# Order of the routing's bookkeeping ahead of the experts: one turn, the ranks, the slot list and the weights are moved

## The chip, the cores and the metric

One core of a Trainium2 chip runs the whole program. The metric is the device time of one execution in microseconds. Three executions of the kernel before gave 2938.93, 2939.79 and 2942.79 us.

## What is computed

Two transformer blocks in float32 on 1024 tokens of width 1024. The second block ends in a hierarchical mixture of experts: 4 groups of 8 experts, the best group for each token, in it the two best experts, 32 experts in all. Cut to what the change touches:

```python
x = x + jnp.matmul(merged, w_out[l])
h2 = rms_norm(x, ffn_norm_g[l])
g_logits = matmul(hf, w_rg) + b_rg ; g_sel = argmax(g_logits)
e_logits = (matmul(hf, w_re) + b_re) of the chosen group
top_p, top_i = lax.top_k(softmax(e_logits), 2)
wts = top_p / sum(top_p) * g_w ; eidx = g_sel * 8 + top_i
# each expert gets its tokens in order, in blocks of 128 rows
row_tok[dest] = token ; row_w[dest] = weight
yb = (silu(xb @ w_g[e]) * (xb @ w_u[e])) @ w_d[e] * wb[:, None]
y.at[row_tok].add(yb)
```

## The kernel before

The order of the work is written out by hand: each stage gives every engine its own program, and semaphores tie them together. Each engine works through its program in order. The change is in one stage, `phase_out_route` (line 2391 on), which lies between the dense products of the second block and the expert stage.

Tokens come in 8 tiles of 128 (TT = 8). For each tile t, TensorE multiplies the merged activations by `w_out` in two halves of 512 columns, `multiply(t, 0)` and `multiply(t, 1)` (L2698 to L2700, 24 matmuls each, in 3 parts for accuracy). VectorE adds the residual (`residual`, L2474) once both halves are there. ScalarE squares and sums (L2659) and takes a root (L2662) in `square(t)`; VectorE finishes the norm (L2486). TensorE turns the normed tile by 8 transposes (`turn(t)`, L2714), ScalarE copies the result out of PSUM (`place(t)`, L2669), and TensorE multiplies it by the router's weights (`logit(t)`, L2723, 16 instructions of 36 columns). On ScalarE `place(t - 1)` stands behind `square(t)`.

VectorE chooses group and experts from the logits for tiles 0 to 4, 5 and 6, and 7, in three calls of `choose`. Its marks are kept in `both` (which experts a token takes) and `run` (sums over tiles). Then:

- The ranks: TensorE multiplies `both` by the triangular `before` (L2742) and `run` by `ones` (L2744), both over 8 x 32 = 256 columns, and sums up the last of `run` (L2747). From these VectorE works out each token's row in its expert's block: `dest`, split into `place_f` and `block_f` (L2467 at 2293.61 us to L2573).
- The weights: five small operations on 8 or 32 elements (L2575 to L2579) that need two exponentials of ScalarE (L2683, L2684).
- The list of slots: 16 one-hot tables `at_place` (128 columns) and a table `told` of 2 x 48 columns for each, which holds the token number (columns 0 to 47) and the token's weight (48 to 95). VectorE builds them in two halves of 8. TensorE multiplies them (L2752, 16 products of 96 columns, 32 instructions in the trace), and VectorE turns the result into `slot_token`, `slot_row` and `slot_weight` (L2596 to L2602). Ahead of that VectorE works out which experts need a further block (`extra_expert`, L2590 to L2594).
- GpSimd waits for `slots` and gathers the rows of the first two experts (L2647).

The expert stage follows in the same programs without a barrier. An expert needs three matrices of 2 MB, each loaded in two halves into one buffer for its kind (gate, up, down). ScalarE rounds a half (L3044), VectorE takes the remainder (L3109, in `lo(GATE)`, `lo(UP)`, `lo(DOWN)`), and this frees the half for the next load (L2769, issued by SyncE). TensorE turns the gathered rows (L2968), ScalarE rounds them (L3060), VectorE takes the remainder (`lo_x`, L3124), and the products follow (L2959). For the first expert the order is:

```python
# VectorE                    # ScalarE              # TensorE
lo(GATE)(0, 0)               hi(GATE)(0, 0)         turn_x(0, 0)
lo_x(0, 0)                   hi_x(0, 0)             product(0, 0, GATE, opened)
lo(UP)(0, 0)                 hi(UP)(0, 0)           product(0, 0, UP, hidden)
```

Of the kernel before, what the change touches and what calls it, by code (L numbers as in the profile page):

```python
# [20 lines left out]
ALU = mybir.AluOpType  # L21
AX = mybir.AxisListType

P = 128
SEQ = 1024
D = 1024
TT = SEQ // P
# [27 lines left out]
NE = NG * EPG  # L55
DE = D // 2
ASSIGN = 2 * SEQ
EXTRA = ASSIGN // P
# [2332 lines left out]
def phase_out_route(c, merged, w_high, w_low, x1_dram, x2, gain_dram, xn_dram, keep_dram, w_group,  # L2391
# [5 lines left out]
    nc = c.nc  # L2397
# [50 lines left out]
    GROUPS_OF = ((0, 5), (5, 7), (7, 8))  # L2448
    logit_bank = lambda t: 7 if t in (5, 6) else 6
    ranks, total = t3(c.ps[:, 0, 0:TT * NE]), c.ps[:, 0, TT * NE:(TT + 1) * NE]  # L2450
    with c.stage(within) as (ctx, block):
        S = lambda n: c.sem(ctx, "or_" + n)
        x_in, params = [S("x_in0"), S("x_in1")], S("params")
# [9 lines left out]
        def _(dve):  # L2463
# [75 lines left out]
            for i in range(TT):  # L2539
# [4 lines left out]
                if i == TT - 2:  # L2544
                    choose(*GROUPS_OF[0])
            choose(*GROUPS_OF[1])
            choose(*GROUPS_OF[2])
            at_step["chosen"] = st.n

            tt(gexp, grp[:, :, 0:NG], gtop[:, :, 0:1].to_broadcast([P, TT, NG]), ALU.subtract)  # L2550
            tt(e2.unsqueeze(2), top[:, :, 1:2], top[:, :, 0:1], ALU.subtract)
# [19 lines left out]
            ts(c.block_no, c.dest, 7, None, ALU.arith_shift_right, ALU.bypass)  # L2571
            W(V.tensor_copy(place_f, c.place_no))
            W(V.tensor_copy(block_f, c.block_no))  # L2573
            dve.wait_ge(act_step, 2)
            W(V.tensor_reduce(gsum, gexp, AX.X, ALU.add))  # L2575
            ts(s2, e2, 1.0, None, ALU.add, ALU.bypass)
            tt(s2, s2, gsum, ALU.mult)
            W(V.reciprocal(c.weight[:, 0:TT], s2))
            tt(c.weight[:, TT:NJ], c.weight[:, 0:TT], e2, ALU.mult)  # L2579
            for j in range(2):  # L2580
                half = slice(j * TT, (j + 1) * TT)
                tt(at_place[:, half, :], bt(iota_f), bl(place_f[:, half], P), ALU.is_equal)
                tt(in_block[:, half, :], bt(iota_f[:, 0:NBLK]), bl(block_f[:, half], NBLK),
                   ALU.is_equal)
                tt(told[:, half, 0:NBLK], in_block[:, half, :], bl(row_f[:, half], NBLK), ALU.mult)
                tt(told[:, half, NBLK:2 * NBLK], in_block[:, half, :], bl(c.weight[:, half], NBLK),
                   ALU.mult)
                at_step["told", j] = st.n

            tt(cmp_, bl(bno, NE), bt(upto, EXTRA), ALU.is_ge)  # L2590
            W(V.tensor_reduce(bex, cmp_, AX.X, ALU.add))
            ts(bex, bex, float(NE - 1), None, ALU.min, ALU.bypass)
            W(V.tensor_copy(c.extra_expert, bex))
            W(V.tensor_copy(c.extra_count, upto[:, NE - 1:NE]))  # L2594
            dve.wait_ge(listed, 1)
            rows = c.ps[:, 1, 0:NBLK]  # L2596
            ts(wrapped, rows, float(SEQ - EMPTY), float(-SEQ), ALU.is_ge, ALU.mult)
# [1 line left out]
                                   op0=ALU.add, op1=ALU.add).then_inc(slots, 1)  # L2599
            W(V.scalar_tensor_tensor(out=c.slot_row, in0=wrapped, scalar=float(EMPTY), in1=rows,  # L2600
                                     op0=ALU.add, op1=ALU.add))
            W(V.tensor_copy(c.slot_weight, c.ps[:, 1, NBLK:2 * NBLK]))  # L2602

        @block.sync
        def _(sp):
# [81 lines left out]
        def _(pe):  # L2687
# [17 lines left out]
            def turn(t):  # L2705
                pe.wait_ge(ready, t + 1)
                for h in range(2):
                    if t:
                        pe.wait_ge(placed, 2 * t + h - 1)
                    else:  # L2710
                        pe.wait_ge(dense.by_vec, EVICTED)
                    for k in range(4):
                        kk = 4 * h + k
                        mm = nc.tensor.transpose(c.ps[:, 4 + h, k * P:(k + 1) * P],  # L2714
                                                 xn[t % 2][:, kk * P:(kk + 1) * P], c.ident[:])
                    mm.then_inc(turned, 1)

            def logit(t):
                pe.wait_ge(placed, 2 * t + 2)
                if t == 0:  # L2720
                    pe.wait_ge(params, 80)
                for k in range(KC):
                    mm = nc.tensor.matmul(c.ps[:, logit_bank(t), t * NL:(t + 1) * NL],  # L2723
                                          hT[:, k, :], w[:, k, :],
                                          start=(k == 0), stop=(k == KC - 1))
                mm.then_inc(logits, 1)

            pe.wait_ge(retired, 1)
            for t in range(TT):
                multiply(t, 0)  # L2730
                if t >= 2:
                    logit(t - 2)
                multiply(t, 1)
                if t:
                    turn(t - 1)
            logit(TT - 2)
            turn(TT - 1)
            logit(TT - 1)
            pe.wait_ge(step, at_step["chosen"])
            for used in experts_may:  # L2740
                pe.sem_inc(used, 1)
            nc.tensor.matmul(c.ps[:, 0, 0:TT * NE], c.before[:], both.rearrange("p t n -> p (t n)"),  # L2742
                             start=True, stop=False, skip_group_check=True)
            nc.tensor.matmul(c.ps[:, 0, 0:TT * NE], c.ones[:],  # L2744
                             run[:, 0:TT].rearrange("p t n -> p (t n)"), start=False, stop=True,
                             skip_group_check=True)
            nc.tensor.matmul(total, c.ones[:], run[:, TT], start=True, stop=True,  # L2747
                             skip_group_check=True).then_inc(ranked, 1)
            for n in range(NJ):
                if n % TT == 0:  # L2750
                    pe.wait_ge(step, at_step["told", n // TT])
                mm = nc.tensor.matmul(c.ps[:, 1, 0:2 * NBLK], at_place[:, n, :], told[:, n, :],  # L2752
                                      start=(n == 0), stop=(n == NJ - 1))
            mm.then_inc(listed, 1)


# [826 lines left out]
```

## Time and profile before

| | us |
|---|---|
| median of three executions | 2939.79 |
| the profiled execution, its own time | 2932.78 |
| its span | 2931.0 |
| TensorE busy | 2756.0 |
| VectorE busy | 1907.3 |
| ScalarE busy | 1442.8 |
| GpSimd busy | 529.9 |
| mean granted TensorE clock | 0.976 |

Times in the trace are microseconds from the start of the span. A granted clock of 1.00 is 2.4 GHz, 0.50 is 1.2 GHz. The routing stage's products run from 2171 to 2275 us, the bookkeeping to about 2310 us, the experts from there to the end. A bracket at the end of a timeline row is how long the engine was idle ahead of it and who released it. Matmuls overlap, so the length of a merged row is from its first start to its last modelled end.

### The profile page before, as it was taken

How to read it: one execution, taken by the hardware profiler on the slowest of the kernel's cores; microseconds unless marked ns; L12 is line 12 of the kernel's file. 1: busy time of each engine (PE TensorE's matmuls, PEld its weight loads, DVE VectorE, ACT ScalarE, POOL GpSimd, SP SyncE). 2: the span in 40 equal slices, each digit the busy share in tenths (PEclk: the TensorE clock that was granted, in tenths of full speed). 3: DMA queues.
4: the chain of work that ended last, by engine and by line, in shares of the span. 5: the costliest groups of instructions: out<-in, count | busy, mean ns of one | idle time of the engine just before them, and what ended most of it. 6: DMA issues, size and time to landing. Idle time of an engine off the chain costs nothing.

```text
span 2931.0 us, 35753 instructions
## 1 busy us (share of the span) xinstructions
PE 2756.0 (94%) x13268; PEld 2251.2 (77%) x13278; DVE 1907.3 (65%) x2187; ACT 1442.8 (49%) x2117; POOL 529.9 (18%) x397
## 2 busy tenths in 40 slices
PE   7999999999998999999989998899899699999997
PEld 6788887888876776887878876778678588888875
DVE  4776836344454664345543987899863699888985
ACT  4444436323336665434333356533532377777774
POOL 0002300000006775001000000000110144334332
PEclk9999999999999999999999998999999799999998
DMA  4110011313456663131211100111222699999995
GB/s 104 44 49 9 16 53 36 108 43 108 165 168 141 153 146 83 44 108 51 87 58 53 44 29 1 30 44 50 93 97 86 226 385 376 371 364 370 363 361 178
DMA packets 162600, 387.92 MB, mean 132 GB/s; under 512 B 72321, under 2 KB 72449, under 8 KB 137888
## 3 DMA queue, kind: packets, MB, share of 16 engines
q1 hardware_dynamic: 151920, 369.13, 37.5%
q0 software_dynamic: 9216, 16.81, 2.3%
q8 instruction: 90, 1.47, 0.2%
q10 hardware_dynamic: 1328, 0.14, 0.0%
q14 instruction: 46, 0.38, 0.0%
HBM read 347.93 MB, written 54.85 MB: 137 GB/s over the span
## 4 chain that ended last, share of the span: by engine, by line
PE 51%; DMA 12%; DVE 10%; POOL 6%; ACT 5%; issue 4%; POOLq 0%; DVEq 0%; SPq 0%; ACTq 0%; PEldq 0%
PE ps L897 12%; PE ps L899 12%; PE ps L898 12%; DMA ex_raw<-in_w_down_e 10%; POOL fa_pl L1336 6%; PE ps L2959 3%; DVE ex_w L3109 3%; DMA ex_raw<-in_w_up_e 2%; ACT ex_w L3044 2%; PE ps L2698 1%; PE ps L1741 1%; PE ps L2700 1%; PE ps L1743 1%; PE ps L1742 1%; PE ps L2699 1%
## 5 line engine op out<-in xcount | busy, mean ns | idle before, releaser
L3109 DVE TENSOR_TENSOR ex_w<-ex_raw,ex_w 128x2048 fp32r<-128x2048 f32 x190 | 430.7, 2289 | 63.4 <-ACT ex_w L3044 61.0
L3044 ACT ACTIVATE ex_w<-ex_raw 128x2048 fp32r<-128x2048 f32 x190 | 362.0, 1916 | 112.9 <-DMA ex_raw<-in_w_up_e 56.8
L2959 PE MATMUL ps<-ex_w,ex_xT 128*128 128x512 f32 x1536 | 367.6, 395 | 13.7 <-DVE ex_xT L3124 13.4
L2959 PEld LDWEIGHTS ps<-ex_w,ex_xT 128*128 128x128 f32 x1536 | 286.9, 189 | 79.5 <-issue 15.1
L1003 DVE TENSOR_TENSOR bs_t<-arena,bs_t 128x1024 fp32r<-128x1024 f32 x88 | 107.8, 1225 | 269.4 <-ACT bs_t L956 269.4
L956 ACT ACTIVATE bs_t<-arena 128x1024 fp32r<-128x1024 f32 x88 | 93.3, 1061 | 294.1 <-PE ps L899 280.3
L793 DVE SCALAR_TENSOR_TENSOR arena<-arena,small 128x1023 f32<-128x1023 f32 (+9 forms) x168 | 213.4, 1271 | 3.5
L1336 POOL TENSOR_TENSOR fa_pl<-fa_p,fa_ph 128x512 fp32r<-128x512 f32 x192 | 196.4, 1041 | 82.0 <-ACT fa_ph L1474 80.4
L2959 PE MATMUL ps<-ex_w,ex_hT 128*128 128x512 f32 x768 | 184.5, 396 | 0.3 <-issue 0.2
L897 PE MATMUL ps<-bs_t,bs_w 128*128 128x512 f32 x448 | 175.3, 391 | 7.8 <-DVE bs_w L994 4.3
L898 PE MATMUL ps<-bs_t,bs_w 128*128 128x512 f32 x448 | 174.4, 389 | 0.0
L899 PE MATMUL ps<-bs_t,bs_w 128*128 128x512 f32 x448 | 174.3, 389 | 0.0
L2959 PEld LDWEIGHTS ps<-ex_w,ex_hT 128*128 128x128 f32 x768 | 143.0, 189 | 30.4 <-issue 1.3
L897 PE MATMUL ps<-gb_t,gb_w 128*128 128x512 f32 x368 | 146.9, 399 | 15.9 <-DVE gb_w L994 8.1
L1003 DVE TENSOR_TENSOR za_t<-arena,za_t 128x1024 fp32r<-128x1024 f32 x48 | 60.1, 1252 | 142.5 <-ACT za_t L956 142.4
L1524 DVE TENSOR_REDUCE small<-ps 128x1 f32<-128x512 f32 (+1 forms) x192 | 100.7, 553 | 78.7 <-PE ps L1361 43.3
L897 PE MATMUL ps<-za_t,za_w 128*128 128x512 f32 x368 | 145.0, 394 | 5.6 <-DVE za_t L1003 3.3
L899 PE MATMUL ps<-gb_t,gb_w 128*128 128x512 f32 x368 | 145.3, 395 | 0.0
L898 PE MATMUL ps<-gb_t,gb_w 128*128 128x512 f32 x368 | 145.1, 394 | 0.0
L898 PE MATMUL ps<-za_t,za_w 128*128 128x512 f32 x368 | 144.2, 392 | 0.0
L899 PE MATMUL ps<-za_t,za_w 128*128 128x512 f32 x368 | 143.9, 391 | 0.0
L1464 ACT ACTIVATE fa_p<-ps 128x512 f32<-128x512 f32 x192 | 94.3, 491 | 88.3 <-PE ps L1401 42.0
(422 smaller groups left out, 6568.2 us busy)
## 6 DMA issues: line engine op xcount, KB each, us to landing
ex_raw<-in_w_gate_e SPq DMA_DIRECT2D x64, 1024.0 KB, 13.7
ex_raw<-in_w_up_e SPq DMA_DIRECT2D x64, 1024.0 KB
ex_raw<-in_w_down_e SPq DMA_DIRECT2D x64, 1024.0 KB, 13.6
arena<-in_w_in SPq DMA_DIRECT2D x108, 512.0 KB, 3.7
att_qk<-bs_split SPq DMA_DIRECT2D x8, 2048.0 KB, 10.8
fa_a<-att_qk SPq DMA_DIRECT2D x32, 256.0 KB
fa_b<-att_qk SPq DMA_DIRECT2D x16, 512.0 KB, 6.5
arena<-in_w_out SPq DMA_DIRECT2D x16, 512.0 KB, 7.1
```

Source lines behind the costliest of these rows:

```text
L793: ins = dve.scalar_tensor_tensor(out=acc[:, b, back:], in0=src[:, b, 0:SEQ - back], scalar=w, in1=acc[:, b, back:], op0=ALU.mult, op1=ALU.add)
L897: nc.tensor.matmul(c.ps[:, t, :], a[0], b[0], start=(k == 0), stop=False)
L898: nc.tensor.matmul(c.ps[:, t, :], a[0], b[1], start=False, stop=False)
L899: mm = nc.tensor.matmul(c.ps[:, t, :], a[1], b[0], start=False, stop=(n == last[j]))
L956: nc.scalar.activation(tp[s][0], jobs[j][0][:, k, :], ACT.Identity).then_inc(t_high, 1)
L1003: V.tensor_tensor(tp[s][1], jobs[j][0][:, k, :], tp[s][0].bitcast(F32), ALU.subtract)\
L1336: nc.gpsimd.tensor_tensor(low[x % 4][:, 0:w], prob[x % 3][:, 0:w], f32(high[x % 4][:, 0:w]), ALU.subtract).then_inc(lowered, 1)
L1464: nc.scalar.activation(prob[x % 3][:, 0:w], c.ps[:, S_BANK[x % 3], 0:w], ACT.Exp)\
L1524: V.tensor_reduce(to, c.ps[:, M_BANK[z % 2], 0:width], AX.X, ALU.max, negate=True)\
L2959: mm = nc.tensor.matmul(out, l, r, start=(k == 0 and n == 0), stop=(k == kc - 1 and n == 2))
L3044: nc.scalar.activation(half_of(part[m][0], h), raw[m][:, h * W // 2: (h + 1) * W // 2], ACT.Identity).then_inc(high[m], 1)
L3109: V.tensor_tensor(half_of(part[m][1], h), raw[m][:, h * W // 2: (h + 1) * W // 2], half_of(as_f32(part[m][0]), h), ALU.subtract)\
```

## The change

`turn(6)` is issued ahead of `multiply(7, 1)` rather than behind it. The rank products are split: tiles 0 to 6 (224 columns) as soon as `choose(5, 7)` is done, tile 7 (32 columns) and the total after `choose(7, 8)`. The five operations for the weights go behind the tables, which are built without the weights. TensorE multiplies the tables twice: first with the 48 columns of token numbers, into bank 1, later with the 48 columns of weights, into bank 7. VectorE makes `slot_token` and `slot_row` after the first, then multiplies the weights into `told`, works out the extra experts, waits for the second listing and copies `slot_weight`.

```diff
--- before.py
+++ after.py
@@ -2448,6 +2448,7 @@
     GROUPS_OF = ((0, 5), (5, 7), (7, 8))
     logit_bank = lambda t: 7 if t in (5, 6) else 6
     ranks, total = t3(c.ps[:, 0, 0:TT * NE]), c.ps[:, 0, TT * NE:(TT + 1) * NE]
+    WEIGHTS = 7
     with c.stage(within) as (ctx, block):
         S = lambda n: c.sem(ctx, "or_" + n)
         x_in, params = [S("x_in0"), S("x_in1")], S("params")
@@ -2544,8 +2545,9 @@
                 if i == TT - 2:
                     choose(*GROUPS_OF[0])
             choose(*GROUPS_OF[1])
+            at_step["chosen", 0] = st.n
             choose(*GROUPS_OF[2])
-            at_step["chosen"] = st.n
+            at_step["chosen", 1] = st.n
 
             tt(gexp, grp[:, :, 0:NG], gtop[:, :, 0:1].to_broadcast([P, TT, NG]), ALU.subtract)
             tt(e2.unsqueeze(2), top[:, :, 1:2], top[:, :, 0:1], ALU.subtract)
@@ -2571,27 +2573,19 @@
             ts(c.block_no, c.dest, 7, None, ALU.arith_shift_right, ALU.bypass)
             W(V.tensor_copy(place_f, c.place_no))
             W(V.tensor_copy(block_f, c.block_no))
+            halves = [slice(j * TT, (j + 1) * TT) for j in range(2)]
+            for j, half in enumerate(halves):
+                tt(at_place[:, half, :], bt(iota_f), bl(place_f[:, half], P), ALU.is_equal)
+                tt(in_block[:, half, :], bt(iota_f[:, 0:NBLK]), bl(block_f[:, half], NBLK),
+                   ALU.is_equal)
+                tt(told[:, half, 0:NBLK], in_block[:, half, :], bl(row_f[:, half], NBLK), ALU.mult)
+                at_step["told", j] = st.n
             dve.wait_ge(act_step, 2)
             W(V.tensor_reduce(gsum, gexp, AX.X, ALU.add))
             ts(s2, e2, 1.0, None, ALU.add, ALU.bypass)
             tt(s2, s2, gsum, ALU.mult)
             W(V.reciprocal(c.weight[:, 0:TT], s2))
             tt(c.weight[:, TT:NJ], c.weight[:, 0:TT], e2, ALU.mult)
-            for j in range(2):
-                half = slice(j * TT, (j + 1) * TT)
-                tt(at_place[:, half, :], bt(iota_f), bl(place_f[:, half], P), ALU.is_equal)
-                tt(in_block[:, half, :], bt(iota_f[:, 0:NBLK]), bl(block_f[:, half], NBLK),
-                   ALU.is_equal)
-                tt(told[:, half, 0:NBLK], in_block[:, half, :], bl(row_f[:, half], NBLK), ALU.mult)
-                tt(told[:, half, NBLK:2 * NBLK], in_block[:, half, :], bl(c.weight[:, half], NBLK),
-                   ALU.mult)
-                at_step["told", j] = st.n
-
-            tt(cmp_, bl(bno, NE), bt(upto, EXTRA), ALU.is_ge)
-            W(V.tensor_reduce(bex, cmp_, AX.X, ALU.add))
-            ts(bex, bex, float(NE - 1), None, ALU.min, ALU.bypass)
-            W(V.tensor_copy(c.extra_expert, bex))
-            W(V.tensor_copy(c.extra_count, upto[:, NE - 1:NE]))
             dve.wait_ge(listed, 1)
             rows = c.ps[:, 1, 0:NBLK]
             ts(wrapped, rows, float(SEQ - EMPTY), float(-SEQ), ALU.is_ge, ALU.mult)
@@ -2599,7 +2593,17 @@
                                    op0=ALU.add, op1=ALU.add).then_inc(slots, 1)
             W(V.scalar_tensor_tensor(out=c.slot_row, in0=wrapped, scalar=float(EMPTY), in1=rows,
                                      op0=ALU.add, op1=ALU.add))
-            W(V.tensor_copy(c.slot_weight, c.ps[:, 1, NBLK:2 * NBLK]))
+            for half in halves:
+                tt(told[:, half, NBLK:2 * NBLK], in_block[:, half, :], bl(c.weight[:, half], NBLK),
+                   ALU.mult)
+            at_step["weighted"] = st.n
+            tt(cmp_, bl(bno, NE), bt(upto, EXTRA), ALU.is_ge)
+            W(V.tensor_reduce(bex, cmp_, AX.X, ALU.add))
+            ts(bex, bex, float(NE - 1), None, ALU.min, ALU.bypass)
+            W(V.tensor_copy(c.extra_expert, bex))
+            W(V.tensor_copy(c.extra_count, upto[:, NE - 1:NE]))
+            dve.wait_ge(listed, 2)
+            W(V.tensor_copy(c.slot_weight, c.ps[:, WEIGHTS, 0:NBLK]))
 
         @block.sync
         def _(sp):
@@ -2725,32 +2729,44 @@
                                           start=(k == 0), stop=(k == KC - 1))
                 mm.then_inc(logits, 1)
 
+            def rank(a, b):
+                out = c.ps[:, 0, a * NE:b * NE]
+                nc.tensor.matmul(out, c.before[:], both[:, a:b].rearrange("p t n -> p (t n)"),
+                                 start=True, stop=False, skip_group_check=True)
+                nc.tensor.matmul(out, c.ones[:], run[:, a:b].rearrange("p t n -> p (t n)"),
+                                 start=False, stop=True, skip_group_check=True)
+
             pe.wait_ge(retired, 1)
             for t in range(TT):
                 multiply(t, 0)
                 if t >= 2:
                     logit(t - 2)
+                if t == TT - 1:
+                    turn(TT - 2)
                 multiply(t, 1)
-                if t:
+                if 1 <= t < TT - 1:
                     turn(t - 1)
             logit(TT - 2)
             turn(TT - 1)
             logit(TT - 1)
-            pe.wait_ge(step, at_step["chosen"])
+            pe.wait_ge(step, at_step["chosen", 0])
+            rank(0, TT - 1)
+            pe.wait_ge(step, at_step["chosen", 1])
             for used in experts_may:
                 pe.sem_inc(used, 1)
-            nc.tensor.matmul(c.ps[:, 0, 0:TT * NE], c.before[:], both.rearrange("p t n -> p (t n)"),
-                             start=True, stop=False, skip_group_check=True)
-            nc.tensor.matmul(c.ps[:, 0, 0:TT * NE], c.ones[:],
-                             run[:, 0:TT].rearrange("p t n -> p (t n)"), start=False, stop=True,
-                             skip_group_check=True)
+            rank(TT - 1, TT)
             nc.tensor.matmul(total, c.ones[:], run[:, TT], start=True, stop=True,
                              skip_group_check=True).then_inc(ranked, 1)
             for n in range(NJ):
                 if n % TT == 0:
                     pe.wait_ge(step, at_step["told", n // TT])
-                mm = nc.tensor.matmul(c.ps[:, 1, 0:2 * NBLK], at_place[:, n, :], told[:, n, :],
+                mm = nc.tensor.matmul(c.ps[:, 1, 0:NBLK], at_place[:, n, :], told[:, n, 0:NBLK],
                                       start=(n == 0), stop=(n == NJ - 1))
+            mm.then_inc(listed, 1)
+            pe.wait_ge(step, at_step["weighted"])
+            for n in range(NJ):
+                mm = nc.tensor.matmul(c.ps[:, WEIGHTS, 0:NBLK], at_place[:, n, :],
+                                      told[:, n, NBLK:2 * NBLK], start=(n == 0), stop=(n == NJ - 1))
             mm.then_inc(listed, 1)
 
 
```

## Rows read from the trace of the kernel before

**Rows 1.** The page of the profile, its first line.

```profile
span 2931.0 us, 35753 instructions
```

**Rows 2.** The chain that ended last: start, length, what.

```profile
2275.27 1.24 DVE arena L2474
...
2278.01 1.07 ACT arena L2669 x2
...
2310.80 4.42 DMA arena<-expert_in,ints
...
2319.62 8.38 PE ps L2959 x24
...
2328.51 1.92 ACT ex_w L3044
...
2342.95 5.50 PE ps L2959 x24
```

**Rows 3.** Timeline of TensorE, 2267 to 2311 us: start, length, what, idle before.

```profile
2267.72 1.87 PE L2723 MATMUL ps<-arena 128*128 128x36 f32 x16
...
2275.00 1.04 PE L2714 MATMUL ps<-ident,arena 128*128 128x128 f32 x8
2279.13 2.07 PE L2723 MATMUL ps<-arena 128*128 128x36 f32 x16 [3.09 <-ACT arena L2669]
...
2283.64 3.63 PE L2723 MATMUL ps<-arena 128*128 128x36 f32 x16 [0.69 <-ACT arena L2669]
2291.20 1.19 PE L2742 MATMUL ps<-arena,before 128*128 128x256 f32 x2 [3.93 <-DVE arena L2467]
...
2293.03 0.47 PE L2747 MATMUL ps<-arena,ones 128*128 128x32 f32 x2
2302.93 6.30 PE L2752 MATMUL ps<-arena 128*128 128x96 f32 x32 [9.42 <-DVE arena L2467]
```

**Rows 4.** Timeline of VectorE, 2293 to 2320 us.

```profile
2293.61 0.39 DVE L2467 TENSOR_TENSOR arena<-ps,arena 128x224 f32<-128x224 f32 x1 [2.43 <-PE ps L2747]
...
2298.80 0.19 DVE L2575 TENSOR_REDUCE arena<-arena 128x8 f32<-128x32 f32 x1
...
2299.87 2.41 DVE L2467 TENSOR_TENSOR arena<-arena 128x1024 f32<-128x1024 f32 x3
2302.31 0.56 DVE L2467 TENSOR_TENSOR arena<-arena,small 128x384 f32<-128x384 f32 x1
...
2305.94 0.69 DVE L2467 TENSOR_TENSOR arena<-arena 128x512 f32<-128x512 f32 x1
...
2309.93 0.21 DVE L2602 COPY small<-ps 128x48 f32<-128x48 f32 x1
2311.04 4.49 DVE L3109 TENSOR_TENSOR ex_w<-ex_raw,ex_w 128x2048 fp32r<-128x2048 f32 x2 [0.90 <-DVE small L2602]
2318.34 1.23 DVE L3124 TENSOR_TENSOR ex_xT<-ps,ex_xT 128x1024 fp32r<-128x1024 f32 x1 [2.80 <-ACT ex_xT L3060]
```

**Rows 5.** Busy time by stretch: busy us of each engine, granted clock, DMA share, GB/s.

```profile
2281.00:2282.00 1.00, 1.00 (x6) 1.00 (x7) 0.66 (x5) 0.00 (x0) 0.03 (x1) 0.50 1.10 315
...
2308.00:2309.00 1.00, 1.00 (x10) 1.00 (x9) 0.00 (x0) 0.00 (x0) 0.00 (x0) 0.91 0.00 0
...
2319.00:2324.00 5.00, 4.38 (x10) 3.47 (x11) 4.43 (x3) 4.18 (x3) 0.38 (x1) 0.50 0.88 329
```

**Rows 6.** Timeline of SyncE's queue, loads of the expert weights.

```profile
2313.36 2.53 SPq L2769 DMA_DIRECT2D ex_raw<-in_w_gate_e  x2
...
2332.77 2.53 SPq L2769 DMA_DIRECT2D ex_raw<-in_w_gate_e  x2
```

**Rows 7.** Busy time by stretch in the expert stage, columns as in rows 5.

```profile
2330.00:2340.00 10.00, 7.57 (x38) 6.26 (x37) 9.03 (x6) 7.88 (x6) 1.64 (x2) 1.00 0.62 213
2340.00:2350.00 10.00, 10.00 (x51) 8.46 (x51) 10.00 (x6) 7.85 (x7) 0.00 (x0) 1.00 1.00 406
...
2400.00:2500.00 100.00, 100.00 (x475) 83.88 (x474) 91.68 (x57) 75.02 (x55) 45.04 (x22) 1.00 1.00 376
```

## Prediction

> **What bounds the kernel now.** I read the chain that ended last first, then the timelines of TensorE and VectorE around it, then clock and DMA by stretch. Up to 2275 us TensorE is the chain: it multiplies without a gap. From 2275.27 to 2328 us the chain is a relay between engines [rows 2]: residual on VectorE, square and copy on ScalarE, logits and turn on TensorE, `choose` on VectorE, ranks on TensorE (2291.20 to 2293.5), the places on VectorE (2293.61 on), the listing on TensorE (2302.93 to 2309.23), the slot numbers on VectorE, the gather (2310.80 to 2315.22), turn, rounding, `lo_x` at 2318.34, the first expert product from 2319.62 to 2328.00, and ScalarE's next rounding at 2328.51 [rows 2 to 4]. A microsecond taken out of that relay comes off the time if no neighbour is late by less. After 2340 us the DMA engines are at a share of 1.00, still at 376 GB/s from 2400 to 2500 us [rows 7]. The loads are throughput bound there, so that stretch is neither shortened nor lengthened by the change: it starts earlier or later, and the end with it. The change is worth what it moves the end of the first product, since its release sets the loads that open the full stretch (below).
>
> **Turn of tile 6, ahead of the last half product.** Before, its 8 transposes run from 2275.00 to 2276.04, and then TensorE sits idle for 3.09 us, until ScalarE's copy of that tile ends at 2279.08 [rows 2, 3]. The copy does not wait for the turn: ScalarE has it behind `square(7)`, which waits for `residual(7)`, which waits for the product of tile 7. So the early turn releases nobody sooner, and it stands ahead of the product on TensorE. Eight transposes at full clock take from 2275.00 to the start of their last at about 0.87 us (1.04 with the last one's tail) [rows 3]; everything from the residual on is 0.87 us later. There is a second part. The clock is at 0.50 from 2281 to 2282 [rows 5]. The 16 instructions of `logit(6)` at 2279.13 were nearly through by then (2.07 us), those of `logit(7)` took 3.63 us, wholly at the half clock, against 1.87 us for the set at 2267.72 [rows 3]. If the fall stays where it is and `logit(6)` starts 0.9 us later, half of it runs at the half clock: half of 3.63 - 1.87, some 0.8 us, at most. I take +1.4 us in all; bounds +0.9 (no part of the clock) and +1.7.
>
> **Ranks of seven tiles early.** Before, VectorE waits from its last mark until 2293.61; TensorE's six instructions start at 2291.20: 2.41 us [rows 3, 4]. After, four of the six have moved behind `logit(7)`, into TensorE's idle 3.93 us [rows 3]; `choose(5, 7)` is long done when `logit(7)` ends. What remains behind the last mark is three pairs of 32 columns, six instructions. No row shows such a six; the nearest is `logit(7)`, 16 instructions of 36 columns in 3.63 us at the same clock, 0.227 each [rows 3], so 1.4 us, and 0.1 to reach VectorE. Gain 0.9 us. Bounds: 0.5 us (the last pair took 0.47 us alone, three of them 1.4, and some setting up is paid again for each pair) and 1.2 us. The cover, if gone, costs the 2 us of the four instructions; `choose(7, 8)` lasts from about 2287.4 to 2291.2 and covers it.
>
> **Weights behind the tables.** The listing starts when the first half of the tables is done. The five operations from 2298.80 to 2299.87 (1.07 us) and the weight product of that half at 2302.31 (0.56 us, 0.60 with its gap) no longer stand ahead of it [rows 4]: 1.67 us. The second half, ready 2.44 us later (three more of the 2.41 us kind, without the 0.60), isn't waited for, because TensorE needs half of 6.30 us for the first [rows 3]. The listing of 48 columns takes how long? At the half clock the 36 column set took 0.227 us an instruction and the 96 column set 6.30/32 = 0.197, with its last microsecond at a clock of 0.91 [rows 3, 5]. So an instruction here costs its weight load and not its columns; I take 6.3 us again. Gain at the slot numbers 1.67 us.
>
> The sum to there: +1.4 - 0.9 - 1.67 = -1.2 us. Slot numbers, gather and the landing of the first rows move from 2315.22 to about 2314.0.
>
> **The second listing, and who queues behind it.** This is the wait that the change adds. From the end of the first listing VectorE needs 0.70 us to the point where the copy stood (2309.23 to 2309.93), then two weight products of 0.60: 1.9 us [rows 4]. TensorE then lists 16 products once more. At the half clock 32 x 0.227 = 7.3 us, at the full one 32 x 1.87/16, 3.7 us [rows 3]; the clock was up from 2308 [rows 5] and TensorE would sit idle 1.9 us only, so I take a mix, 5.2 us. The extra experts' numbers (five operations, from 2305.94, about 2.0 us [rows 4]) hide behind it, as they hid behind the first. Then the copy (0.3 with its release) and the 0.90 us that stood ahead of `lo(GATE)` [rows 4]. So `lo(GATE)` starts 1.9 + 5.2 + 1.2 = 8.3 us behind the first listing's end, where it was 2311.04 - 2309.23 = 1.8: +6.5 us, and with the -1.2 above, +5.3 us. VectorE takes its work in order: `lo(GATE)` holds it for 4.5 us, and `lo_x`, for which the first product waits, stands behind. Before, it had 2.80 us to spare there [rows 4]. Of +5.3 us, +2.5 is left on `lo_x` and on the product.
>
> TensorE has a queue of its own to watch: `turn_x` stands behind the second listing, which ends at about 2315.1 (2309.23 - 1.2 + 1.9 + 5.2), 1.1 us after the rows have landed. Turn, rounding and their releases took from 2315.27 to 2318.34; this leads to some 2318.2, ahead of the 2320.8 at which VectorE is free. So VectorE's order decides, not this.
>
> The first product ran from 2319.62 to 2328.00, mostly at the half clock (0.50 over 2319 to 2324) [rows 2, 5]. It will start some 2.5 us later, after about 4 us of idle TensorE, and so I leave its length. The Trainium skill ("TensorE: Matmul & The Clock Gate", "What's actually happening") says that activity releases the throttle; the trace agrees, 0.91 at 2308 after five microseconds of listing [rows 5].
>
> **Loads.** SyncE's load of the second expert's gate matrix at 2313.36 waits for the first half of `lo(GATE)` and comes 5.3 us later. The load that matters is the one at 2332.77 [rows 6]: it waits for VectorE's remainder behind ScalarE's 2328.51 [rows 2], so for the first product. Between the two the DMA engines have slack (share 0.62 from 2330 to 2340) [rows 7]. So the lateness of the full stretch is the product's, +2.5 us. On GpSimd nothing new is queued; `scatter` needs `slot_weight` only through the experts' outputs, much later.
>
> **Sum.** The profiled execution took 2932.78 us, its span is 2931.0 [rows 1], so 1.8 us lie around it; it would become 2935.3. The median lies 7.0 us above the profiled one; the change adds the same to it: 2939.8 + 2.5 = 2942.3 us.
>
> **Rivals.**
> (a) *The loads start late and stay late.* If the full stretch hangs on the load at 2313.36 and not on the one at 2332.77, all of the +5.3 us counts, and with the second listing wholly at the half clock 2.1 us more: 2947.2, slower by 0.25%. For it: DMA is the bound for most of the stage. Against it: the idle share before 2340 [rows 7]. It decides once the second expert's gate lands after the first product's end, that is if `lo(GATE)` is some 7 us late. Chance 0.12.
> (b) *The clock stays up.* TensorE now works on either side of 2310 us. If the second listing runs at the full clock (-1.5), the first one gets it earlier too (-1.2) and the product runs mostly at 2.4 GHz (8.38 us against the 5.50 that 24 such matmuls take at 2342.95 [rows 2]: -2.9), the time is 2942.3 - 5.6 = 2936.7. For it: 0.91 at 2308. Against it: gaps of 3 and 4 us stay in this relay, and the clock was at 0.50 two microseconds after the one of 3.09 [rows 3, 5]. Chance 0.13 for most of it.
> (c) *A listing costs its columns.* Then 2 x 48 columns cost what 96 did: 3.15 us each. The first ends 1.6 us after the second half of the tables, at 4.0 us instead of 6.3 from its start (-2.3), the second takes 3.15 rather than 5.2 (-2.0): 2938.0. Rows 3 speak against it. The Trainium skill ("TensorE: Matmul & The Clock Gate", "Step-by-step: what each phase is for") would have it so: throughput is purely N cycles. By its section "LDWEIGHTS (loading the stationary operand)", with a cost by the 128 stationary columns, it would be 6.3 us each time, as I took from the rows. Chance 0.10.
> (d) The forecast, +1 to +4.5 us with the bounds of its terms: 0.60. The remaining 0.05 is for disturbance of the DMA-bound stretch in either direction.
>
> **Range and chances.** 0.2%, 5.9 us, is about what a measurement of this kernel can tell from no change. Faster by more (below 2933.9) needs (b) in full and more: 0.05. Slower by more (above 2945.7) is (a) and the edge of (d): 0.13. Within: 0.82. The range reaches from (b) to (a), 2936 to 2947.5, where the three executions of before alone span 3.9 us.
>
> **What would show it.** Right: in the trace after, `residual(7)` some 0.9 us later; six small rank instructions in about 1.5 us after the last mark; `slot_token` about 1 us earlier; two rows of 32 at the listings' line, the second several microseconds long; `lo(GATE)` directly behind it, with no idle time between it and `lo_x`; the full DMA stretch starting 2 to 3 us later. Wrong: idle time left on VectorE ahead of `lo_x` (then the gather still decides, and the gain stands at about -1.2 us), a listing of under 4 us at the half clock (c), or a first product of under 6 us (b).

## The result and the profile after

The changed kernel takes 2943.98 us (median of 20 executions, 2936.89 to 2950.8), the kernel before 2938.53 in the same comparison (20 executions); the ratio is 1.0021, 95% interval 1.0011 to 1.0030. So it is slower by 3 to 9 us, 6 at the centre, where the forecast had +2.5. The profiled execution has a span of 2938.3 us against 2931.0 [rows 1].

Executions of one and the same kernel differ by up to 15 us, and in the traces most of that arises ahead of the changed code: the logits of tile 5 start at 2268.17 us in one trace of the changed kernel and at 2277.22 in a second, whose time is 7.6 us longer. So traces are compared by places counted from that start (2267.72 before, 2268.17 after).

The timeline of TensorE in the changed kernel (start, length, what, idle before):

```profile
2280.38 3.03 PE L2727 MATMUL ps<-arena 128*128 128x36 f32 x16 [3.96 <-ACT arena L2673]
...
2302.62 7.06 PE L2763 MATMUL ps<-arena 128*128 128x48 f32 x32 [7.76 <-DVE arena L2468]
2311.59 7.06 PE L2768 MATMUL ps<-arena 128*128 128x48 f32 x32 [1.91 <-DVE arena L2468]
2319.65 1.95 PE L2984 MATMUL ps<-ident,arena 128*128 128x128 f32 x8 [0.99 <-DVEq L3186]
...
2341.60 7.36 PE L2975 MATMUL ps<-ex_w,ex_xT 128*128 128x512 f32 x24 [2.43 <-DVE ex_xT L3140]
```

The idle time ahead of `logit(6)` has grown from 3.09 to 3.96 us, and its length from 2.07 to 3.03 [rows 3]. Both listings (L2763 the token numbers, L2768 the weights) take 7.06 us. The timeline of VectorE:

```profile
2276.53 1.22 DVE L2475 TENSOR_TENSOR arena<-ps,arena 128x1024 f32<-128x1024 f32 x1 [3.20 <-PE ps L2704]
...
2294.97 0.39 DVE L2468 TENSOR_TENSOR arena<-ps,arena 128x224 f32<-128x224 f32 x1 [1.58 <-PE ps L2758]
...
2309.80 0.21 DVE L2469 TENSOR_SCALAR arena<-ps 128x48 f32<-128x48 f32 x1 [3.71 <-PE ps L2763]
...
2318.76 0.21 DVE L2606 COPY small<-ps 128x48 f32<-128x48 f32 x1 [5.17 <-PE ps L2768]
2319.87 4.49 DVE L3125 TENSOR_TENSOR ex_w<-ex_raw,ex_w 128x2048 fp32r<-128x2048 f32 x2 [0.90 <-DVE small L2606]
2324.28 1.22 DVE L3140 TENSOR_TENSOR ex_xT<-ps,ex_xT 128x1024 fp32r<-128x1024 f32 x1
```

VectorE waits 5.17 us for the second listing ahead of the copy (L2606). `lo_x` (L3140) stands directly behind `lo(GATE)` (L3125), and the 2.80 us that VectorE had to spare there are gone [rows 4]. The granted clock is 0.50 all through both listings and the start of the first product (stretches, columns as in rows 5):

```profile
2308.00:2310.00 2.00, 1.69 (x8) 1.52 (x8) 0.20 (x1) 0.00 (x0) 0.00 (x0) 0.50 0.00 0
...
2326.00:2328.00 2.00, 2.00 (x6) 1.54 (x6) 2.00 (x2) 1.54 (x2) 0.00 (x0) 0.50 1.01 385
```

### The profile page after: what moved, and what is told of

Read it like the earlier page. It is cut to its first block, busy times and chain, and to the rows that moved or that the text cites. A ratio compares the mean times of both kernels' runs of the same rounds, so it can differ in the third digit from the quotient of the medians.

```text
span 2938.3 us, 35826 instructions
## 1 busy us (share of the span) xinstructions
PE 2763.0 (94%) x13304; PEld 2258.3 (77%) x13314; DVE 1906.6 (65%) x2187; ACT 1442.4 (49%) x2117; POOL 538.0 (18%) x397
## 4 chain that ended last, share of the span: by engine, by line
PE 53%; DMA 12%; DVE 9%; POOL 5%; ACT 5%; issue 4%; POOLq 0%; SPq 0%; DVEq 0%; ACTq 0%; PEldq 0%
PE ps L897 12%; PE ps L899 12%; PE ps L898 12%; DMA ex_raw<-in_w_down_e 11%; POOL fa_pl L1336 5%; PE ps L2975 4%; DVE ex_w L3125 2%; ACT ex_w L3060 2%; PE ps L2702 1%; PE ps L1741 1%; PE ps L2704 1%; PE ps L1743 1%; PE ps L2703 1%; PE ps L1742 1%; DVE gb_t L1003 1%
## 5 line engine op out<-in xcount | busy, mean ns | idle before, releaser
L3125 DVE TENSOR_TENSOR ex_w<-ex_raw,ex_w 128x2048 fp32r<-128x2048 f32 x190 | 430.3, 2288 | 64.1 <-ACT ex_w L3060 61.6
L3060 ACT ACTIVATE ex_w<-ex_raw 128x2048 fp32r<-128x2048 f32 x190 | 361.3, 1916 | 105.4 <-DMA ex_raw<-in_w_up_e 55.9
L1524 DVE TENSOR_REDUCE small<-ps 128x1 f32<-128x512 f32 (+1 forms) x192 | 100.8, 553 | 80.9 <-PE ps L1361 43.5
L1464 ACT ACTIVATE fa_p<-ps 128x512 f32<-128x512 f32 x192 | 94.2, 491 | 90.5 <-PE ps L1401 42.9
```

The costliest lines, as they stand in the source:

```text
L1464: nc.scalar.activation(prob[x % 3][:, 0:w], c.ps[:, S_BANK[x % 3], 0:w], ACT.Exp)\
L1524: V.tensor_reduce(to, c.ps[:, M_BANK[z % 2], 0:width], AX.X, ALU.max, negate=True)\
L3060: nc.scalar.activation(half_of(part[m][0], h), raw[m][:, h * W // 2: (h + 1) * W // 2], ACT.Identity).then_inc(high[m], 1)
L3125: V.tensor_tensor(half_of(part[m][1], h), raw[m][:, h * W // 2: (h + 1) * W // 2], half_of(as_f32(part[m][0]), h), ALU.subtract)\
```

## Where each kernel stands

Places in us from the start of the logits of tile 5, each a start in the kernel's own trace: the first rank product behind the last mark, VectorE's first operation on the ranks, the first listing, `slot_token`, `lo(GATE)` and `lo_x` of the first expert, the loads of the third and the fifth expert's gate matrix. The last column is the time as a ratio to the kernel before. A place comes from one trace, a ratio from 10 executions or more. The traces of before and late_load, kernels that differ only in a wait of SyncE, agree in all these places within about 0.1 us.

| | mark | ranks used | listing | slots | lo(GATE) | lo_x | load 3 | load 5 | ratio (95%) |
|---|---|---|---|---|---|---|---|---|---|
| before | 23.5 | 25.9 | 35.2 | 41.9 | 43.3 | 50.6 | 65.1 | 97.9 | |
| changed | 25.2 | 26.8 | 34.5 | 41.9 | 51.7 | 56.1 | 69.5 | 104.0 | 1.0021 (1.0011 to 1.0030) |
| changed, again | 25.2 | 26.7 | 34.4 | 41.8 | 51.6 | 56.0 | 69.4 | 104.0 | one execution |
| turn_only | 25.0 | 27.4 | 36.8 | 44.3 | 45.7 | 52.9 | 66.2 | 100.8 | 1.0012 (0.9994 to 1.0030) |
| ranks_only | 23.8 | 25.3 | 34.6 | 41.4 | 42.9 | 50.2 | 64.7 | 97.6 | 1.0009 (0.9992 to 1.0025) |
| split_only | 23.9 | 26.3 | 33.9 | 41.3 | 51.2 | 55.6 | 69.1 | 103.6 | 1.0025 (1.0006 to 1.0044) |
| late_copy | 25.8 | 27.4 | 35.1 | 42.5 | 46.9 | 53.9 | 67.3 | 101.8 | 1.0009 (0.9994 to 1.0023) |
| listing_late | 25.8 | 27.4 | 35.0 | 42.5 | 46.9 | 51.3 | 67.1 | 102.2 | 1.0000 (0.9989 to 1.0011) |
| late_load | 23.6 | 26.0 | 35.3 | 41.9 | 43.3 | 50.5 | 65.0 | 97.9 | 0.9999 (0.9986 to 1.0013) |
| before_warm | 22.4 | 24.0 | 33.3 | 40.7 | 42.1 | 48.7 | 62.3 | 96.7 | 0.9989 (0.9973 to 1.0006) |
| after_warm | 23.4 | 24.2 | 31.9 | 38.3 | 45.1 | 49.5 | 62.6 | 97.1 | 0.9993 (0.9975 to 1.0011) |
| early_weights | 23.2 | 25.1 | 32.2 | 40.3 | 41.7 | 48.9 | 62.5 | 97.0 | 0.9981 (0.9966 to 0.9996) |
| warm | 22.4 | 23.7 | 30.8 | 38.9 | 40.3 | 46.7 | 61.3 | 94.2 | 0.9987 (0.9972 to 1.0003) |

My theory was VectorE's order: the copy waits for a second listing, and the first expert's work stands behind it. The rivals were the turn with the clock (the earlier turn and the longer logits are the loss), and the late loads (the second expert's weights come too late, and all that follows with them).

## The parts of the change, one at a time

**turn_only**

```diff
+                if t == TT - 1:
+                    turn(TT - 2)
                 multiply(t, 1)
-                if t:
+                if 1 <= t < TT - 1:
```

> Only the turn of tile 6 is moved ahead of the last half product. Places are counted from the start of the logits of tile 5 in the same trace (2267.72 us before, 2268.17 after). If the turn costs what stands on TensorE ahead of the product and the clock's fall stays in place: residual of tile 7 later by 0.8 us, last mark (start of the rank products) at 25.2 to 25.3 us against 23.48 before, that is +1.8, the first expert product +1 to +2 us, the time +1 to +2 us (2939.5 to 2940.5). Rival, that the late loads and not the turn cause what is seen in this stretch: last mark unmoved, 23.5.

The last mark comes 1.55 us later. `logit(6)`, with 3.96 us of idle time ahead of it as in the changed kernel, takes 2.82 us; the listing takes 7.14 us, all at the half clock, and the slot numbers are 2.4 us late. The turn alone loses 2.3 us at `lo_x` and at the first product, a little more than the +1 to +2 I expected: 0.8 of it is the listing, which takes 7.14 where it took 6.30. The ratio's interval is compatible with that and does not tell it from nothing.

**ranks_only**

```diff
+            pe.wait_ge(step, at_step["chosen", 0])
+            rank(0, TT - 1)
+            pe.wait_ge(step, at_step["chosen", 1])
...
+            rank(TT - 1, TT)
```

> Only the rank products are split, the ones of seven tiles early. VectorE's wait from the start of the last mark's products to its next operation 1.56 us against 2.41; the slot numbers at 41.0 us from the logits of tile 5 against 41.86, the first expert product 0.8 us sooner by both theories, time -0.8 us, not to be told from no change in the times.

The wait is 1.57 us. `logit(6)` took 2.36 us here, 0.3 longer than before, and the listing 6.42, 0.1 longer, so the gain at the first product is 0.5 and not 0.85 us.

**split_only**: the changed kernel with the turn and the ranks put back, so that of the change only the two listings are left.

```diff
-                if t == TT - 1:
-                    turn(TT - 2)
                 multiply(t, 1)
-                if 1 <= t < TT - 1:
+                if t:
                     turn(t - 1)
...
-            pe.wait_ge(step, at_step["chosen", 0])
-            rank(0, TT - 1)
-            pe.wait_ge(step, at_step["chosen", 1])
+            pe.wait_ge(step, at_step["chosen"])
```

> Only the listing is split: tables without weights, second listing, extra experts' numbers last; turn and ranks as before. Theory of VectorE's order (the copy of the slot weights waits for the second listing, and lo(GATE) and lo_x stand behind it): listing starts 1.67 us sooner, VectorE's lo(GATE) 7.5 us later than before, no idle time between it and lo_x, first expert product +4.5 to +6 us, time +4 to +6 us. Rival theory (the turn and the clock in the logits are the loss): first expert product -0.5 to -1.7 us, time not above before.

The listing starts 1.3 us sooner by the table, 1.7 sooner counted from the last mark, but `lo(GATE)` is 7.9 us late and `lo_x` 5.0, without idle time between them. That is nine tenths of the changed kernel's +5.5 at `lo_x`, and the one part whose time is clear of no change (its interval is +2 to +13 us). The rival that the turn is the main loss falls; its 2.3 us are a part. The three parts, +2.3, -0.5 and +5.0, add up to 6.8 and not to 5.5. Turn_only and split_only both contain the 0.8 us by which a listing wholly at the half clock is longer, and it is paid once in the changed kernel; most of the rest is `logit(6)`, whose length differs from trace to trace (2.36 and 2.46 us in ranks_only and split_only against 2.07 before). VectorE in this kernel:

```profile
2319.08 0.21 DVE L2605 COPY small<-ps 128x48 f32<-128x48 f32 x1 [5.17 <-PE ps L2760]
2320.19 4.49 DVE L3117 TENSOR_TENSOR ex_w<-ex_raw,ex_w 128x2048 fp32r<-128x2048 f32 x2 [0.90 <-DVE small L2605]
2324.60 1.22 DVE L3132 TENSOR_TENSOR ex_xT<-ps,ex_xT 128x1024 fp32r<-128x1024 f32 x1
```

## Who is held by the second listing

**late_copy**

```diff
-            dve.wait_ge(listed, 2)
-            W(V.tensor_copy(c.slot_weight, c.ps[:, WEIGHTS, 0:NBLK]))
...
                 lo_x(*after)
                 lo(UP)(*after)
+                if after is FIRST and not extra:
+                    c.late()
```

`c.late` holds the wait and the copy that are taken out above.

> The changed kernel, but VectorE waits for the second listing and copies the slot weights only behind lo(UP) of the first expert. TensorE's order is unchanged: turn_x still stands behind the second listing. Theory of VectorE's order alone: lo(GATE) starts at 2314.5 us in the changed kernel's places instead of 2319.87, VectorE is idle ahead of lo_x, and lo_x is 2.3 to 2.6 us sooner, then held by TensorE, whose second listing ends at 2318.65 and whose turn follows at once; the rest, some 3 us against before, remains, and shows that the second listing costs on two engines. If it was VectorE only, lo_x would be 5 us sooner. Rival (late loads set the lateness): the second expert's gate load comes 5.4 us sooner, and the time falls by 5 us or more. Expected time 2941 to 2942.

```profile
2328.26 4.49 DVE L3128 TENSOR_TENSOR ex_w<-ex_raw,ex_w 128x2048 fp32r<-128x2048 f32 x2 [0.90 <-DVE ints L2604]
2335.25 1.23 DVE L3143 TENSOR_TENSOR ex_xT<-ps,ex_xT 128x1024 fp32r<-128x1024 f32 x1 [2.50 <-ACT ex_xT L3079]
```

These are VectorE's rows. The idle time ahead of `lo_x` is back, 2.50 us, and its releaser is ScalarE, which waited for the turn. `lo_x` is 2.2 us sooner than in the changed kernel, although this trace has `logit(6)` in 3.63 us and so 0.6 us more up to the slots. The expectation of the theory holds but for 0.1 us, also in its second half: 3.3 us against before remain. The second expert's gate load comes 4.8 us sooner than in the changed kernel (49.24 us against 54.02), the third only 2.2, as `lo_x`: a first sign against the late loads. In TensorE's rows the turn follows the second listing at once:

```profile
2325.36 7.06 PE L2771 MATMUL ps<-arena 128*128 128x48 f32 x32 [1.91 <-DVE arena L2468]
2332.22 1.93 PE L2987 MATMUL ps<-ident,arena 128*128 128x128 f32 x8
```

**listing_late**

```diff
             if now:
                 product(*now, GATE, opened)
+                if now is FIRST and not extra:
+                    c.list_weights()
```

`c.list_weights` holds TensorE's wait and the 16 products of the second listing, which are taken out of the routing stage. The late copy is as above.

> The changed kernel with both late: TensorE multiplies the weights' listing behind the gate product of the first expert, and VectorE copies the slot weights behind lo(UP) of the first expert. In the run with the late copy alone lo_x still came 3.3 us later than before, held by the turn behind the second listing. If that rest is the second listing on TensorE, lo_x now comes at 50.6 us from the logits of tile 5, within 0.8 us of the kernel before, and turn_x at 47.5; the load of the third expert's gate at 65 us within 1. The listing then costs the up product 3.5 to 7 us, of which a wait of 2.4 us ahead of the next product hides a part. Rival (something else in the changed kernel holds the turn, as the gather): turn_x stays at 50 us or more.

`lo_x` comes at 51.3, 0.7 us behind the kernel before, of which 0.6 stand at the slots already. So the rest was the second listing on TensorE, and the two engines together account for the whole loss at `lo_x`. `lo(GATE)` is still 3.6 us later than before (46.9 us), since the two weight products and the extra experts' numbers now stand behind the slot numbers; VectorE's spare time covers that, and none of it is left. The second listing takes 3.67 us here, at a granted clock of 1.00. But load 3 comes 1.1 us later than the latest that I expected:

```profile
2345.54 0.21 DVE L2607 COPY small<-ps 128x48 f32<-128x48 f32 x1 [6.92 <-PE ps L2773]
2345.78 4.50 DVE L3135 TENSOR_TENSOR ex_w<-ex_raw,ex_w 128x2048 fp32r<-128x2048 f32 x2
```

The copy now holds `lo(GATE)` of the second expert, whose rounded half was ready from ScalarE, and with it the load. The same fault one expert later, put there by my own edit. Place and time do not agree for this kernel: load 5 is 4.3 us late, while the ratio of 1.0000 allows 3 us at most (its lowest time, 2935.56 us, is 5.5 above the lowest of the kernel before in the same comparison, 2930.09). That stays open, and so the times do not show what the late listing is worth.

**late_load**

```diff
+            if now is FIRST:
+                sp.wait_ge(x_low, 2)
             if after and after is not FIRST:
                 load(*after, (GATE, UP))
```

> The kernel before, but SyncE waits for lo_x of the first expert ahead of the load of the second expert's gate matrix, so that this load is issued 6.2 us later (51.9 us from the logits of tile 5 against 45.64), as it was by 8.4 us in the changed kernel. Nothing else is changed. If the load at that place does not set the end (my step on the loads), the first product, the load of the third expert's gate (65.05) and the time stay where they are, within 0.5 us in the trace. Rival (the loads start late and stay late): the third gate load and all that follow come up to 6 us later, time +4 to +6 us.

SyncE's queue in this kernel, where the logits of tile 5 start at 2276.97:

```profile
2328.76 0.80 SPq L2769 DMA_DIRECT2D ex_raw<-in_w_gate_e  x2
2331.63 2.53 SPq L2769 DMA_DIRECT2D ex_raw<-in_w_up_e  x2
2341.95 2.53 SPq L2769 DMA_DIRECT2D ex_raw<-in_w_gate_e  x2
```

The second gate load is issued 6.2 us later than before [rows 6] and the third at 65.0 as before; so is the fifth. The ratio is 0.9999. In the changed kernel this load is 8.4 us late, more than the 6.2 here, but its chain that ended last does not wait for a load either. ScalarE's operation on the first product (L3080), its rounding of the second expert's gate matrix (L3060) and VectorE's remainder follow the product at once:

```profile
2332.88 0.02 ACT arena L3080
...
2333.38 1.92 ACT ex_w L3060
```

The rival of the late loads falls, and the step that put the start of the full DMA stretch on the first product stands.

## The clock

**before_warm**: the kernel before, with products in TensorE's waits whose result nobody reads.

```diff
+            def filler(n, bank):
+                for _ in range(n):
+                    nc.tensor.matmul(c.ps[:, bank, 0:P], c.ident[:], c.ones[:], start=True,
+                                     stop=True, skip_group_check=True)
+            pe.wait_ge(added, TT - 1)
+            filler(11, 1)
             logit(TT - 2)
             turn(TT - 1)
             logit(TT - 1)
+            filler(11, 5)
```

31 more stand behind the ranks and 17 behind the listing.

> The kernel before, with idle products (ident by ones, 128 columns, result never read) in TensorE's waits: 11 behind the turn of tile 6, 11 behind the logits of tile 7, 31 behind the ranks, 17 behind the listing. Theory that the relay pays for the half clock: granted clock 1.00 through the relay, logits of tiles 6 and 7 in 1.9 us each, listing in 3.5 to 4 us and then held by VectorE's second half of the tables, first product in 5.5 us; the load of the third expert's gate matrix at 55 to 57 us from the logits of tile 5 against 65.05, time lower by 6 to 10 us. Rival, that the idle products stand in the way or do not hold the clock: logits of tile 7 still 3.6 us and the listing delayed by up to 7 us.

```profile
2280.00:2282.00 2.00, 2.00 (x14) 2.00 (x14) 1.76 (x12) 0.79 (x1) 0.00 (x0) 0.65 0.89 348
2282.00:2284.00 2.00, 2.00 (x11) 2.00 (x11) 1.58 (x10) 0.00 (x0) 0.00 (x0) 0.50 1.00 418
```

In these stretches of its trace TensorE is busy throughout and the clock falls; ahead of them it had idled for 0.63 and 0.80 us at the two copies of ScalarE, no more. It rose again at about 2287.4 (0.64 over 2286 to 2288, 1.00 behind), after TensorE had been busy without a gap since 2279.6, and fell at about 2297.7 (0.92 over 2296 to 2298, 0.50 behind), at the end of 2.41 us of idle time. `logit(7)` took 2.69 instead of 3.63 us, the listing 7.02. The expectation of a clock of 1.00 throughout failed, and with it the 6 to 10 us. `lo_x` is 1.9 us sooner and load 3 2.8, the later loads 1.2; the ratio is not clear of 1.

**after_warm**: the same on the changed kernel (13 ahead of `logit(6)`, 7 and 26 around the last ranks, 5 between the listings).

> The changed kernel with the same kind of idle products: 13 ahead of the logits of tile 6, 7 behind the early ranks, 26 behind the ranks, 5 between the two listings. If my sum missed by the clock alone, both listings take 3.5 to 4 us, the logits of tile 6 1.9 us, and lo_x comes no later than in the kernel before with its half clock (50.6 us from the logits of tile 5, within 1.5); against the kernel before with idle products the loss of the first expert product is 2 to 4 us. If it missed by VectorE's order, lo_x stays 5 us behind the kernel before with idle products.

Here the listings took 6.09 and 3.81 us and `logit(6)` 1.98. `lo_x` comes at 49.5, within 1.5 us of the kernel before, and only 0.8 us behind before_warm, so less than the 2 to 4 I expected. But its slot numbers are 2.3 us sooner than those of before_warm (38.3 us against 40.7). Counted from the slot numbers, `lo_x` comes after 8.8 us before and 14.2 changed, 5.5 more; after 8.0 in before_warm and 11.2 here, 3.1 more. VectorE still waits 2.07 us ahead of the copy and has no idle time ahead of `lo_x`. So the second listing's cost on the path is 2.4 us less where it takes 3.81 instead of 7.06 us; the larger part of it, 3.1 us, remains at the higher clock as long as the copy waits where it does.

## A version that beats both

**early_weights**: the kernel before, with the early ranks; the weights worked out in VectorE's wait for the ranks; tables and the one listing of 96 columns in quarters. TensorE's semaphore steps for the experts go behind the rank products. The edit, cut to the weights and the quarters:

```diff
+            dve.wait_ge(act_step, 2)
+            W(V.tensor_reduce(gsum, gexp, AX.X, ALU.add))
...
             dve.wait_ge(ranked, 1)
...
-            for j in range(2):
-                half = slice(j * TT, (j + 1) * TT)
+            for j in range(4):
+                half = slice(j * TT // 2, (j + 1) * TT // 2)
```

> The kernel before with the early ranks; the token weights worked out in VectorE's wait for the ranks; tables and one listing of 96 columns in quarters; TensorE's semaphore steps for the experts behind the rank products. VectorE resumes 1.0 to 1.2 us sooner, the listing starts 3.5 to 3.8 us sooner (31.5 us from the logits of tile 5 against 35.21), the slot numbers and the first product 2.8 to 3.7 us sooner; time -3 us. Rival (loads set the end): the load of the second expert's gate comes 3 us sooner too, so this run alone does not tell them apart; nothing else waits.

The listing starts 3.0 us sooner but takes 7.74 us, partly waiting for VectorE's quarters; the slot numbers gain 1.6 us and load 3 2.6 us, less than I had expected, but no second listing is paid. Ratio 0.9981 (0.9966 to 0.9996). Which of its four edits gains what was not taken apart; the early ranks alone gain 0.5 us at the slot numbers (ranks_only). Once more, for a narrower interval:

**early_repeat**

> The kernel with early weights and quarters once more, for a narrower interval: ratio 0.998 to 1.000, that is 0 to 6 us below the kernel before; by its trace (the third gate load 2.6 us sooner, the later ones 1 to 1.5) some 2 us.

Ratio 0.9986 (0.9974 to 0.9998), `lo_x` at 49.1, load 3 at 62.5, load 5 at 97.0. This is 0.6 to 7.6 us below the kernel before, by the trace some 1 to 2.5.

**warm**: the same with idle products (11, 7, 22, 17).

> The same kernel as the one with early weights and quarters, with idle products in TensorE's waits: 11, 7, 22 and 17. With the clock up: slot numbers at 34 to 36 us from the logits of tile 5, first product in 5.5 us, load of the third expert's gate at 54 to 56 us against 65.05, time -9 to -11 us. If the idle products stand in the way: slot numbers later than without them.

The loads come 3.7 us sooner than before and stay so up to load 5; the slot numbers missed my 34 to 36 (38.9), since the clock was at 0.50 again for much of the listing (2302 to 2306 us in this trace, where the listing runs from 2298.22 to 2305.96). Load 3 at 61.3 us misses the 54 to 56, and the time the -9 to -11 us. In the time (0.9987, 0.9972 to 1.0003) nothing is gained over early_weights that could be told.

**after_repeat**: the changed kernel once more.

> The changed kernel once more, for a second trace. If the lengths of the small products go by where the clock falls, logits of tile 6 and the listings differ from the first trace (3.03 and 7.06 us) by up to 1 us and lo_x lies between 55 and 57 us from the logits of tile 5. If they are fixed costs, all are within 0.1 us.

Places agree within 0.1 us and `logit(6)` took 2.96 us. Two traces that agree do not show a spread by the clock; the range of `logit(6)` in other kernels with the same idle time ahead (2.82 in turn_only, 3.63 in late_copy) does.

## Why the prediction was right in direction and short in size

The range (2936 to 2947.5) held the 2943.98, and the loss came where it was put. Point by point:

- **The number.** The 2943.98 lies 1.7 us above the forecast, but the change is 5.5 us (of the medians) where +2.5 was forecast, and above the +4.5 that the bounds of the terms allowed. The sum started from 2939.8, the median of three executions; 20 gave 2938.53. That base was 1.3 us high, and that the total came so near is in that part luck.
- **The turn.** Residual +0.81 for +0.87: right. The clock's part, about 0.5 and at most 0.8, was 0.96 (3.03 - 2.07). Last mark +1.76 for +1.4, just past the bound of +1.7.
- **The ranks.** 1.56 us for 2.41: -0.85 for -0.9.
- **The start of the listing.** 34.45 from the logits, with +1.76 and -0.85 ahead of it: -1.67, as summed.
- **The listing's length.** 6.3 put, 7.06 measured, since the clock no longer rose in it. With it the slot numbers stand where they stood (41.87 for 41.86); of the -1.2 us nothing was left.
- **The second listing.** 5.2 put, 7.06 measured. This is the largest miss, a mix of clocks chosen between 3.7 and 7.3 where the half clock held.
- **VectorE's order.** 2.80 us to spare, then late: right. The sum at `lo_x` was +2.5; adding 0.4, 0.8 and 1.9 for the three terms of the clock gives 5.6, and the trace has +5.5. All mis-sized terms are one: how long TensorE would run at 1.2 GHz. That is the step that failed; the waits and their order came as forecast.
- **The first product.** Its start is +5.5 and the third gate load +4.4, since it was 1.1 us shorter (7.31 us, 8.38 before); the fifth gate load is +6.0, since the product at 2341.60 took 7.36 us where the one after the same 2.43 us of idle time before took 5.74. I had left both out.
- **Rivals.** (a) falls by late_load and by the changed kernel's chain, though the +6.0 at the fifth gate load is of its size. (b) did not occur in the changed kernel; with idle products it did in part. (c) falls: at the half clock 32 instructions of 48 columns took 7.06 us and of 96 columns 7.14 (turn_only). The Trainium skill ("TensorE: Matmul & The Clock Gate", "LDWEIGHTS (loading the stationary operand)") prices the load of the stationary operand by its 128 columns. These two rows agree in that the moving columns do not set the length, but they do not agree with its formula in size: for 128 columns that gives an estimate of 0.107 us, near the 0.115 us of an instruction at the full clock (3.67 us for 32, listing_late) and half of the 0.22 at the half clock. By the formula a listing would be 3.4 us, and not the 6.3 that the prediction names beside the section.

What I missed besides: in the changed kernel the turn waits another 0.99 us, released by VectorE's queue at L3186, a semaphore step that stands behind the copy. It cost nothing, as VectorE was later still.

## What to carry to other kernels

Work taken off one chain is paid again if it is split into a second pass with as many instructions as the first, where an instruction costs the same whatever its columns. A wait for its result belongs behind everything in the queue that others need. For a relay between engines, price TensorE's small products at both clocks and sum each way; do not mix. Look first for work that fits into a wait that already exists.

## What was not expected of the hardware

- With idle products in TensorE's waits the clock still fell to 0.50, within a stretch busy 2.00 of 2.00 us and with only gaps of 0.63 and 0.80 us ahead of it (before_warm, 2280 to 2282). These runs do not settle why.
- 16 instructions of 36 columns took 1.87 to 3.63 us by where the clock fell; those of `logit(6)` 2.07, 2.36 and 2.46 in kernels that are identical up to there (before, ranks_only, split_only).
- The two traces of the changed kernel reach this stage 9 us apart. All of it is there at the matmul that starts at 300 us in the first: the granted clock over 0 to 100 us is 0.98 in one and 0.93 in the other, over 200 to 300 us 0.98 and 0.91. Why the clock differs there is open.
